# Preparing weight blocks two ahead instead of one, where a slot and a stage are free

## The reference, cut to what matters

```python
# first block, once
mod = silu(c) @ w_ada + b_ada                     # 6 vectors of 1024
h = rmsnorm(x) * (1 + sc1) + sh1
proj = h @ w_in                                   # beta, alpha, q, k, v, conv inputs, z
y = concat(dilated_attention(q, k, v), gated_deltanet(...)) @ w_out
x = x + g1 * y
x = x + g2 * ((silu(h2 @ w_gate) * (h2 @ w_up)) @ w_down)     # d_ff 2816
# second block, 2 layers, each on main (512) and context (256) tokens
m, mc = silu(c) @ w_ada + b_ada, silu(c_ctx) @ w_ada + b_ada  # 9 vectors of 1024 each
h = h + 0.5 * gate * swiglu(modulate(rms_norm(h)))            # half-step ffn1
z = modulate(rms_norm(h)) @ w_in                              # mixer sections
h = h + gate * mix_heads(z, ...) @ w_out
h = h + 0.5 * gate * swiglu(...)                              # half-step ffn2
```

## Time and profile before

| | |
|---|---|
| median of 3 runs | 4035.07 us (4033.82 to 4037.08) |
| profiled execution | 4036.63 us, of which span 4034.6 us |
| PE busy | 3673.1 us, 91% |
| DVE busy | 2287.4 us, 57% |
| ACT busy | 1058.9 us, 26% |
| DMA | 348.33 MB, mean 86 GB/s |
| PE clock granted | mean 0.946 of full |

### The profile page before, as it was taken

The page is one execution under the profiler, slowest core; times in us unless marked ns, Lnnn a source line. Parts: engine busy times, 40 slices in busy tenths (PEclk is TensorE's granted clock), DMA queues, the critical chain, the costliest instruction groups (busy, mean ns, idle before and its releaser), DMA issues. The chain is left out here.

```text
span 4034.6 us, 47247 instructions
## 1 busy us (share of the span) xinstructions
PE 3673.1 (91%) x19008; PEld 2966.7 (74%) x19008; DVE 2287.4 (57%) x5186; ACT 1058.9 (26%) x1633; POOL 216.9 (5%) x189
## 2 busy tenths in 40 slices
PE   5899998999889999977889999998999997789997
PEld 3755886788778888765547888887888885457886
DVE  5564556755666666755355666676666535434334
ACT  2354002322331111233242212123112123233222
POOL 1012101000010000100100000010000011000000
PEclk9998887999989999988989999998999998899999
DMA  5532003344323333333102333332333313012332
GB/s 160 152 97 72 1 1 86 112 119 119 104 65 97 105 103 107 91 96 95 46 16 84 95 105 94 110 100 79 95 110 96 97 49 88 27 42 84 94 94 68
DMA packets 663803, 348.33 MB, mean 86 GB/s; under 512 B 29989, under 2 KB 658919, under 8 KB 663328
## 3 DMA queue, kind: packets, MB, share of 16 engines
q1 hardware_dynamic: 662432, 342.69, 30.3%
q10 hardware_dynamic: 1152, 2.62, 0.2%
HBM read 340.55 MB, written 4.72 MB: 86 GB/s over the span
## 5 line engine op out<-in xcount | busy, mean ns | idle before, releaser
L1733 PE MATMUL psum<-hn_high,high 128*128 128x512 f32 (+2 forms) x3360 | 1231.1, 366 | 114.3 <-DVE hn_low L2139 62.3
L1735 PE MATMUL psum<-hn_high,low 128*128 128x512 f32 (+2 forms) x3360 | 1204.3, 358 | 0.0
L1734 PE MATMUL psum<-hn_low,high 128*128 128x512 f32 (+2 forms) x3360 | 1200.6, 357 | 0.0
L1733 PEld LDWEIGHTS psum<-hn_high,high 128*128 128x128 f32 (+1 forms) x3360 | 639.6, 190 | 245.0 <-DVE hn_low L2139 85.5
L1735 PEld LDWEIGHTS psum<-hn_high,low 128*128 128x128 f32 (+1 forms) x3360 | 639.0, 190 | 102.8 <-issue 1.2
L1734 PEld LDWEIGHTS psum<-hn_low,high 128*128 128x128 f32 (+1 forms) x3360 | 640.8, 191 | 93.1 <-issue 1.5
L2108 DVE TENSOR_TENSOR low<-stage,high 128x1024 fp32r<-128x1024 f32 (+3 forms) x440 | 523.9, 1210 | 186.0 <-ACT high L1439 185.4
L2164 DVE SCALAR_TENSOR_TENSOR partial<-stage,cond,partial 128x128 f32<-128x128 f32 x2304 | 625.1, 346 | 0.0
L1439 ACT ACTIVATE high<-stage 128x1024 fp32r<-128x1024 f32 (+3 forms) x440 | 437.0, 1016 | 504.8 <-DMA stage<-in_w_ffn 364.8
L1733 PE MATMUL psum<-hidden_high,high 128*128 128x512 f32 (+1 forms) x1408 | 502.1, 357 | 3.9 <-DVE low L2108 3.9
L1735 PE MATMUL psum<-hidden_high,low 128*128 128x512 f32 (+1 forms) x1408 | 494.1, 351 | 0.0
(11 more groups left out here) (304 smaller groups left out, 3145.0 us busy)
## 6 DMA issues: line engine op xcount, KB each, us to landing
stage<-in_w_ffn SPq DMA_DIRECT2D x240, 512.0 KB, 4.4
stage<-in_w_ada SPq DMA_DIRECT2D x192, 512.0 KB, 4.0
stage<-in_w_in SPq DMA_DIRECT2D x56, 512.0 KB, 5.2
stage<-in_w_out SPq DMA_DIRECT2D x32, 512.0 KB, 4.2
stage<-in_w_ffn SPq DMA_DIRECT2D x32, 384.0 KB, 3.9
stage<-in_w_gate SPq DMA_DIRECT2D x22, 512.0 KB, 3.9
stage<-in_w_up SPq DMA_DIRECT2D x22, 512.0 KB, 5.1
stage<-in_w_down SPq DMA_DIRECT2D x16, 512.0 KB, 4.2
```

The lines of the kernel that those rows point to most:

```text
L1733: self.e.matmul(out, high[:, i], xh, start=first and i == 0, stop=False)
L1734: self.e.matmul(out, high[:, i], xl, start=False, stop=False)
L1735: done = self.e.matmul(out, low[:, i], xh, start=False, stop=last and i == nk - 1)
```

## The change

`weights` now looks one block further (`n + 5` in place of `n + 4`) and takes the second split block ahead as target in place of the first. `bring_to` brings a block that isn't asked for yet only if the next stage, and for a split block the next slot, isn't taken at that point of the walk; otherwise it stops. `peek` is new and tells which spot comes next. "Taken" is a state of the walk (whose freeing instruction has not been written yet), not a time on the chip.

```diff
 class Turn:
+    def peek(self):
+        return self.spots[self.n % len(self.spots)]
+
     def next(self):
-        s = self.spots[self.n % len(self.spots)]
+        s = self.peek()
         self.n += 1
...
         if split:
-            later = [m for m in range(n + 1, min(n + 4, len(plan))) if plan[m][5]]
-            target = later[0] if later else n
+            later = [m for m in range(n + 1, min(n + 5, len(plan))) if plan[m][5]]
+            target = later[1] if len(later) > 1 else later[0] if later else n
         self.bring_to(target)
         return n, *self.ready_blocks.pop(n)
 
     def bring_to(self, target):
         while self.brought <= target:
+            if self.brought >= len(self.asked):
+                split = self.board.plan[self.brought][5]
+                if self.stages.peek().taken or split and self.slots.peek().taken:
+                    return
             self.ready_blocks[self.brought] = self.bring(self.brought)
             self.brought += 1
```

## The result

| | before | after |
|---|---|---|
| median of the runs | 4034.78 us (4033.82 to 4037.08, 4 runs) | 4315.01 us (4308.79 to 4319.97, 4 runs) |
| profiled execution | 4036.63 us, span 4034.6 | 4319.97 us, span 4318.1 |
| PE clock granted, mean | 0.946 | 0.921 |

The ratio is 1.0693, with a 95% interval of 1.0677 to 1.0709: 280 us slower. The forecast was 4337 us in a range of 4180 to 4440. Lines of the kernel after are 6 higher than those of before in this part: `high` is 1445, `low` 2114, the products 1739 to 1741, the modulation's matmul 1761 and its sums 2170.

A forecast was written before the change was run, and what follows sets the result against it. The prediction took PE, busy 91% of the span, as the bound. From the profiled 4036.6 us, 348 us of losses less 46 of gain gave 4338.6, or 4337 us against the median, forecast range 4250 to 4430 (4180 to 4440 including the absorbed stall).

The forecast's parts named there:

- alpha's step: Step around the gate rows: pair issued behind beta's sums, 6.7 us with hardly any cover; 7 us lost.
- q, k, v, first conv step: First block, q2 to q7, v0 to v3, first conv step: 11 steps of 3.9 us, three about 1 less; 40 lost.
- conv: Conv steps: 11 x (4.9 mean stall + 2 for a slower PE clock), 76 us lost.
- w_out: w_out steps: 4.6 us each, 1.2 + 6 x 4.6 + 2.3 = 31 us lost.
- six 8-tile groups: 8-tile down steps with modulation blocks: +3.6 us a full step, 24.6 a group, 148 us lost.
- two 6-tile groups: 6-tile down steps: +3.6 us a step, 23 us a group, 46 us lost.
- gain: Mixers, down steps and out steps behind a context norm: fewer PE waits for `low`, 46 us won (25 to 60).
- The clock elsewhere: Stretches other than conv: PE has slack to run at either clock level, so nothing added.
- What the trace would show: 8-tile down step: `high` about 6 us after the pair, DVE waiting 3.6, steps 12.4, PE waiting 3 to 4.
- The partly absorbed stall: Rival, alternating steps: pair lands sooner, some 2.2 us a step, conv 3; 4190 us, chance 0.10.
- The clock as the bound: Rival: pauses in some 90 steps bring 1.2 GHz, PE bounds at about 6 us a step; 4470 us, chance 0.06.
- an unchanged order: Rival, modulation stretches: guard stops at a stage a modulation block holds, only mixers gain; 3989 us, chance 0.07.

The follow-up runs named there:

- alone 78: Kernel after with two blocks ahead only in the 12 conv steps, one ahead elsewhere: 4114.32 us, +78 over before.
- both kinds alone: 175: Kernel after with two blocks ahead only in down steps of half-steps with main and context, one ahead elsewhere: 4211.63 us, 175 us over before.
- alone 48: Kernel after with two blocks ahead only where no modulation block lies between, one ahead elsewhere: 3986.88 us, ratio 0.9878.
- the fifth experiment: Kernel after with loads and ACT's `high` still two blocks ahead, but DVE's `low` back to one ahead: 4076.97 us, ratio 1.0096.

## Why the prediction came out right

The mechanism held at each step: the guard let both blocks through, the pair left at the end of the sums, the `low` moved ahead of the next sums, and the loop sums, transfer, `high`, `low` set the pace. The sum was some 20 us too high, and no single term carries it. By terms (measured by the shift between the two traces, in us):

| term | forecast | measured |
|---|---|---|
| alpha's step | 7 | 3.4 |
| q, k, v, first conv step | 40 | 40 |
| conv | 76 | 80, alone 78 |
| w_out | 31 | 29 |
| six 8-tile groups | 148 | 141 |
| two 6-tile groups | 46 | 41 (both kinds alone: 175) |
| gain | 46 | 48, alone 48 |
| **sum** | **302** | **286 by these terms, 283.5 by the spans** |

- *8-tile down step, 3.6 us.* It took 12.5 us in place of 8.8: +3.7. The groups gave 20 to 26 us each where 24.6 were forecast.
- *6-tile down step, 3.6 us: too high.* SP's times after, one step apart:

```profile
1872.46 0.37 SPq L447 DMA_DIRECT2D stage<-in_w_ada  x1
...
1883.54 0.37 SPq L447 DMA_DIRECT2D stage<-in_w_ada  x1
```

  The step takes 11.1 us (the one before it 11.3); in the kernel before it took 8.2 (1672.17 and 1680.38 are two such points, the second in rows 5). So +2.9. The delay of the `low` was sized right: it stands 6.0 us behind the pair in place of 2.5, +3.5. What I had not looked at is that DVE's own work in the step got shorter: from the `low` to the next pair 5.1 us in place of 5.7. Before, it ran beside POOL's sums of squares; after, POOL is done before the `low` begins. POOL and DVE before, then DVE after:

```profile
1683.14 1.46 POOL L1381 TENSOR_TENSOR mean_ctx<-mean_ctx,tmp 128x256 f32<-128x256 f32 x1
...
1683.92 0.95 DVE L2161 TENSOR_SCALAR partial<-stage,cond 128x128 f32<-128x128 f32 x2
```

```profile
1879.36 0.48 DVE L2167 TENSOR_SCALAR partial<-stage,cond 128x128 f32<-128x128 f32 x2
```

  3.5 - 0.6 = 2.9. That POOL is the cause is read from these two traces and not tested. In the 8-tile step POOL does nothing, DVE's part is 5.3 us in both kernels, and the whole delay is paid.
- *q, k and v step, 3.9 us.* The steps took 9.9 us (SP's pairs at 165.85 and 175.75) in place of 6.0: right.
- *w_out step, 4.6 us.* 9.9 us (778.77, 788.64) in place of 5.9 (two pairs of before, 666.66 in rows 8 the first): +4.0. The `low` comes 6.65 us after the pair, not 7.0, and itself takes 1.2 us in place of the 1.46 of rows 8, which began beside POOL's sum (668.17 to 669.45).
- *Conv, 4.9 + 2 for the clock.* The split of the sum was right, in both parts: 49.6 us of idle time against 54, and 28.4 us of slower work against 22. The reason for the first part was only half right. I took DVE's delay as the rule and ACT's as one step in three; the fifth experiment shows ACT's alone makes 68 of 78 us. The two sizes were near each other (4.4 and 6.0 us in the prediction), so the sum didn't show it: that this term came out near its size is in part luck.
- *Alpha's step, 7 us.* +3.4. I said "hardly any cover". There was some: PE's wait for the gate rows, 9.8 us before, grew by only 3.2.
- *Gain, 46 us.* 48 alone. The waits for `low` in the mixers went away altogether and did not just fall to "under 20"; part came back as 21 us of waits for `tmp` instead of as waits at u0, and 12.5 us were gained in PE's busy time. The total was right, its parts were not.
- *The clock elsewhere.* "PE has the slack to run at either level": the window above shows 1.4 us a step of slower work that made no difference to the 12.5.
- *What the trace would show.* DVE's wait in the down step was forecast at 3.6 us and is 6.04. The step's price is 3.7 all the same: the 2.08 us in which DVE waited for PE fell away, since PE's sums are done by then, and moved into the one wait. PE's waits for `partial` were forecast at 3 to 4 us a step and were 1.9 to 2.5: the steps had the forecast length, but PE's work filled 10.1 us of them and not 8.8.
- *The rivals.* The partly absorbed stall would have wanted the pair to land sooner, and it landed 5.7 to 6.1 us after it left, as before, and not in the 4.4 us of the estimate. The clock as the bound didn't come, nor did an unchanged order.

## What to carry to other kernels

A wait that is moved forward in a queue is only free if its transfer's start moves forward too. Before looking further ahead, follow for one period of the pattern which event frees the buffer that the new load takes, and what is queued ahead of it on the issuing engine: here a load two blocks ahead still hung on the last sums, because the buffers were taken strictly in turn with blocks that live longer. The price of a step is the new loop less the old step, not the difference between two places in a queue, and deeper lookahead should be switched on only where the consumer is seen waiting.

## What the runs showed of the hardware

- Two 512 KB loads issued 0.42 us apart: the first lands some 4 us and the second 5.7 to 6 us after the pair left. Alone, such a load lands in 3.8 us. Halving the first brings the second's landing forward by 1.0 us.
- Pauses of PE of 4 to 7 us, one in each conv step, went with a granted clock of 0.79 in place of 0.99, and cost PE 28 us on 130 us of unchanged work. In the down steps, with 2.4 us idle in each, it was 0.91.
- A wait of PE of 2.5 us was followed by 3.3 us at a granted clock of 0.50 (18 matmul records in place of 28); behind one of 1.4 us at the same place of the program the clock stayed at 1.00. In the down steps of the change the clock fell behind waits of 2.54 us (at 1448.59) and 1.89 us (at 1461.11), and not behind one of 1.95 us (at 1473.71).
- Two of DVE's `TENSOR_SCALAR` took 0.95 us beside an instruction of POOL and 0.48 without, and a split of 1024 columns 1.46 us in place of 1.22. POOL's own instruction took 1.46 us there and 0.73 without DVE.
